# Where a 6 MB table of bucket lines is written to memory, in a two-block transformer kernel

## What is computed

```
for l in range(2):                              # first block
    h = rms_norm(x, pre_mix_norm[l]); proj = h @ w_in[l]
    mix = concat(neighbourhood(...), diff(...), gqa(...), mla(...)) @ w_o[l]
    x = x + rms_norm(mix, post_mix_norm[l])
    h = rms_norm(x, pre_ffn_norm[l])
    gate, up = split(h @ ffn_w_gate_up[l])
    x = x + rms_norm((silu(gate) * up) @ ffn_w_down[l], post_ffn_norm[l])
                                                # second block: attention with a bias by distance
bias = rel_table[rel_bucket(query - key)]       # 32 buckets, 16 heads
lg = q @ k.T * scale + bias                     # masked causally or to a band
```

## Time and profile before

| | us |
|---|---|
| median of 3 runs | 2453.93 (2448.55 to 2456.43) |
| profiled execution, device time | 2451.02 |
| its span | 2449.1 |
| PE busy | 2374.7 (97%) |
| DVE, ACT, POOL busy | 482.9, 387.4, 110.5 |
| HBM written, of 565.87 MB moved | 9.18 MB |

### The profile page before, as it was taken

The page is one execution under the profiler, slowest core; times in us unless marked ns, Lnnn a source line. Parts: engine busy times, 40 slices in busy tenths (PEclk is TensorE's granted clock), DMA queues, the critical chain, the costliest instruction groups (busy, mean ns, idle before and its releaser), DMA issues.

```text
span 2449.1 us, 34374 instructions
## 1 busy us (share of the span) xinstructions
PE 2374.7 (97%) x15191; PEld 1363.2 (56%) x15191; DVE 482.9 (20%) x1206; ACT 387.4 (16%) x951; POOL 110.5 (5%) x190
## 2 busy tenths in 40 slices
PE   7999999999999999999999988999999999999997
PEld 4777775778675767877676663333333333333332
DVE  3340002341001532200114431011101010111012
ACT  1420000241000252100015221111111111111110
POOL 3210100010000020100001000000000000000000
PEclk9999999999999999999999999999999999999999
DMA  9567633624425254342444346999999999999993
GB/s 296 206 65 193 230 120 116 244 67 146 166 102 184 83 215 155 134 172 103 135 144 148 112 146 237 382 389 337 369 393 378 347 367 391 374 353 369 391 371 150
DMA packets 245575, 568.15 MB, mean 232 GB/s; under 512 B 10336, under 2 KB 22816, under 8 KB 245424
## 3 DMA queue, kind: packets, MB, share of 16 engines
q1 hardware_dynamic: 233392, 532.24, 59.4%
q0 software_dynamic: 12032, 33.67, 6.0%
HBM read 556.69 MB, written 9.18 MB: 231 GB/s over the span
## 4 chain that ended last, share of the span: by engine, by line
PE 94%; DVE 2%; ACT 2%; issue 1%; DMA 1%; DVEq 0%; POOL 0%; SPq 0%; ACTq 0%
PE ps_d L1374 16%; PE ps_x L1401 8%; PE ps_s L1374 8%; PE ps_a L1163 8%; PE ps_d L1163 8%; PE ps_a L969 6%; PE ps_a L944 6%; PE ps_x L1180 5%; PE ps_s L1180 5%; PE ps_x L1407 4%; PE ps_s L1012 3%; PE ps_x L1012 3%; PE ps_x L1079 3%; PE ps_a L1147 2%; PE ps_d L1147 2%; PE ps_a L1061 1%
## 5 line engine op out<-in xcount | busy, mean ns | idle before, releaser
L1401 PE MATMUL ps_x<-slots,PT 128*32 128x512 f32 x1792 | 212.9, 593 | 0.8 <-ACT PT L1795 0.8
L1163 PE MATMUL ps_a<-hT,slots 128*128 128x256 f32 x864 | 192.7, 382 | 3.9 <-issue 3.9
L1374 PE MATMUL ps_d<-slots,hT 128*32 128x512 f32 x1792 | 195.8, 593 | 0.6 <-ACT hT L1745 0.6
L1374 PE MATMUL ps_d<-slots,N 128*32 128x512 f32 x1792 | 196.0, 593 | 0.0
L1163 PE MATMUL ps_d<-hT,slots 128*128 128x256 f32 x864 | 190.9, 379 | 0.0
L1163 PEld LDWEIGHTS ps_a<-hT,slots 128*128 128x128 f32 x864 | 165.4, 192 | 31.6 <-issue 9.9
L1163 PEld LDWEIGHTS ps_d<-hT,slots 128*128 128x128 f32 x864 | 164.5, 190 | 22.0
L969 PE MATMUL ps_a<-hT,slots 128*128 128x256 f32 (+1 forms) x768 | 143.4, 348 | 1.9 <-ACT hT L1617 1.5
L2503 DVE TENSOR_TENSOR proj<-proj,ps_d 128x512 f32<-128x512 f32 x33 | 22.7, 687 | 596.4 <-PE ps_d L1163 525.1
L969 PEld LDWEIGHTS ps_a<-hT,slots 128*128 128x128 f32 x768 | 126.9, 192 | 18.7 <-issue 5.6
L1401 PEld LDWEIGHTS ps_x<-slots,PT 128*32 128x32 f32 x1792 | 58.3, 110 | 132.8 <-issue 132.8
(11 more groups left out here) (371 smaller groups left out, 2374.5 us busy)
## 6 DMA issues: line engine op xcount, KB each, us to landing
slots<-in_moe_w_gate SPq DMA_DIRECT2D x56, 2048.0 KB, 9.6
slots<-in_moe_w_up SPq DMA_DIRECT2D x56, 2048.0 KB, 10.9
slots<-in_moe_w_down SPq DMA_DIRECT2D x56, 2048.0 KB, 11.2
slots<-in_ffn_w_gate_up SPq DMA_DIRECT2D x20, 2048.0 KB, 11.2
slots<-in_ffn_w_down SPq DMA_DIRECT2D x10, 2048.0 KB, 9.0
slots<-in_w_in SPq DMA_DIRECT2D x8, 2048.0 KB, 9.2
slots<-in_ff_w_gate SPq DMA_DIRECT2D x5, 2048.0 KB, 9.0
slots<-in_ff_w_up SPq DMA_DIRECT2D x5, 2048.0 KB, 8.5
```

The lines of the kernel that those rows point to most:

```text
L1163: last = pe.matmul(b[:, f * S:(f + 1) * S], v[:, k, (f0 + f) * P:(f0 + f + 1) * P], hT[:, k, :], start=(k == 0), stop=(k == KD - 1))
L1374: last = pe.matmul(b[TILE * j:TILE * j + TILE, :], x_of[i][:, k, TILE * c:TILE * c + TILE], views[w][:, k, :], start=(k == 0), stop=(k == ...
L1401: last = pe.matmul(b0[TILE * j:TILE * j + TILE, :], mine(f + o, c), v[:, f + o, 512 * half:512 * half + 512], start=(first and o == 0), st ...
```

## The change

The entry `lines` of Pool's list is no longer made at the first feed-forward. It is made at the stage whose `diff` is the last layer, that is, the second layer's attention, behind that stage's biases. The two transfers, their sources, their targets and their semaphore stay as they are.

```
-                first_ffn = [kind for kind, _ in stages].index("ffn") if any(k == "ffn" for k, _ in stages) else -1
                 for n, (kind, s) in enumerate(stages):
-                    if n == first_ffn:
-                        todo.append(("lines", n, None))
                     if kind == "small":
                         todo.append(("small", n, s["l"]))
...
                     for b in sorted({j["bias"] for u in s.get("units", []) for j in u["jobs"] if j["bias"] is not None}):
                         todo.append(("bias", n, b))
+                    if s.get("diff") == DEPTH - 1:
+                        todo.append(("lines", n, None))
```

## The result

The changed kernel takes 2478.48 us (median of 4 runs, 2475.8 to 2483.13), the kernel before 2453.48 beside it. The ratio is 1.0099, with a 95% interval from 1.0081 to 1.0118: some 25 us slower; 2477 was forecast. The profiled execution went from a span of 2449.1 to 2474.0, +24.9.

What follows compares the result with a forecast made beforehand. TensorE (PE), 94% of the chain, was taken to bound the kernel. 28.6 + 1.9 - 5.8 = +24.7 us gave 2475.7 on the profiled execution, 2478.6 by the median; forecast 2477, range 2463 to 2494.

Steps and rivals of the forecast that it cites:

- Place and order: Pool issues the write about 486.5 us, after the second layer's last distance bias; vectors and `mem` queue behind and land late.
- the sum: Whole kernel: 28.6 us PE delay, plus 1.9 slow clock, minus 5.8 saved in the first feed-forward, +24.7 us.
- First feed-forward, -5.8: First layer's feed-forward: PE's 3.89 us wait at 242.44 and 1.92 us of slow matmuls after it both go.
- Stall, +28.6: Second layer's feed-forward starts at 586.9 instead of 558.27, since PE waits for the late `mem` and vector: +28.6 us.
- My list of what the changed profile would show: Expected signs: write issued about 486.5, vector near 88 us to landing, PE idle 554.7 to about 583, no wait at 242.
- Clock behind the wait, +1.9: After PE's wait before the second layer's feed-forward, a lower clock costs 1.9 us, as after the earlier short wait.
- No vector passed the write: Rival: vectors and `mem` behind the write land before 543, so no stall; 2445 or 2448 us; chance 0.06.
- The second transfer does not get faster in an empty place: Rival claimed the opposite: it spreads over all engines without weights, write ends at 549; 2449 to 2452 us; chance 0.05.
- My reading that it is slow because it runs on half of the engines: The write's second transfer, 8 lines, runs on 8 of 16 engines at half the rate, taking another 41 us.
- The larger stall: Rival: weights and write disturb each other more, `mem` lands after 600, PE waits 45 us or more; 2495 and above; 0.06.
- my upper bound: Largest PE delay, +42 us: 28.6, plus 5 for weights beside the write, plus 8 for SP's loads ahead of `mem`.

Runs made afterwards that it cites:

- the vector alone: Changed kernel with both gain vectors still behind the write on Pool's queue, but `mem` loaded by SP on its own queue: 2476.38 us, ratio 1.01.
- `mem` alone: Changed kernel with the write issued behind the second layer's two gain vectors and ahead of `mem`: 2475.47 us, ratio 1.0089.
- nothing urgent behind the write: Changed kernel with the two gain vectors issued ahead of the write and `mem` loaded by SP on its own queue: 2465.79 us, ratio 1.0052.

## Why the prediction was right

**Place and order: right.** The write at 481 (486.5 less what the first feed-forward gives back), the vector 86.2 us to landing, `mem` behind it, PE idle in front of the turn of `mem`. The two conditions that the sum named (the vector and `mem`, both late) were tested each by itself. Each nearly carries the loss: the feed-forward starts 3.3 us earlier with the vector alone, and PE waits 2.7 us less with `mem` alone. For the vector the reason is partly another than I gave: ScalarE's order holds up the turn of `mem` too.

**First feed-forward, -5.8: measured -5.8** there (no wait, and 1.92 us less for the 32 matmuls). The changed kernel's execution had come to it 0.8 us later than that of the kernel before, and its last distance bias is issued 5.6 us earlier (485.12 to 479.52). That the wait was the write's is confirmed twice: it goes when the write is made fast in its old place, and comes back one layer later with the write behind `mem`. In the time of whole runs the gain is not seen.

**Stall, +28.6.** PE's wait measured 22.4 us, and yet the feed-forward began where the sum puts it. The sum lets everything come 5.8 us earlier: `mem` lands at 583.2 - 5.8 = 577.4, and it landed at 577.2. The end of the output projection should have come 5.8 us earlier too, at 548.8. It came at 554.9, since PE lost 5.2 us in the attention beside the write: the gap of 2.29 us, one of 0.84, and slow clock behind them. The sum has nothing for that; this term is wrong. It changes the place where the time is lost and not the end, because PE starts again when `mem` has landed, whatever it lost before. Where the wait is short, as with nothing urgent behind the write, most of it shows in the time. My list of what the changed profile would show has the write at 486.5 and `mem` at 583, without the 5.8 us, so there the times are 6 us too late.

That `mem`'s landing comes out within 0.2 us is in part luck. The second transfer landed 84.4 us after its issue and not 87.2, and the vector and `mem` landed 2.9 and 10.8 us behind it, where I had 1.9 and 8.4.

**Clock behind the wait, +1.9: measured +1.7** (577.28 to 582.69 for what took 554.57 to 558.27). From Pool's last distance bias on, the measured terms are -5.6, then +5.8 to the end of the output projection, +22.4 and +1.7, together 24.3; the feed-forward begins 24.4 us later, and the span is 24.9 longer.

**The rivals.** No vector passed the write. The second transfer does not get faster in an empty place. My reading that it is slow because it runs on half of the engines was half wrong: it does run so, but on all of them it is no faster. The source's partitions set the rate, for both transfers; of the source as the limit the prediction had said that it was my reading, and the source on 128 partitions shows it. The larger stall did not come: `mem` landed 10.8 us behind the write, so the competing loads of SP cost at most 2.4 us beyond my sum, where my upper bound had 8.

**Not forecast:** the gaps in the attention. They sit at the same matmuls of L1048 in all five kernels that reach them at normal clock with the slow write beside (2.2 to 2.8 us), and in none of the seven without the slow write there; in the run with only the first transfer, where PE came to this point some 12 us late and at the lower clock, there is none. In all five, a packet of an instruction queue is carried within a microsecond of the gap's start (at 501.5 us in the changed kernel), and PE goes on some 2 us later. The kernel before carries such a packet beside the same matmuls, at 507 us, and PE does not stop. The packet itself takes no longer beside the write (0.9 us, 1.3 before). That the write delays the arrival of PE's instructions is a possible cause; it was argued from this, not tried, and what would be held up is not shown.

## What to carry to other kernels

Before a transfer is moved to a quiet place, list what is issued behind it on the same queue, up to the first thing that a busy engine waits for, and take the landing times of loads that already stand behind such a transfer in the trace. Look at the rate and not only at the engines' busy share: 102 GB/s at a share of 0.96 says that the source or the target is narrow, and a source spread over all partitions made the write 3.5 times faster, after which none of three places tried cost anything measurable. A gain of 5 us in 2450 is not to be trusted from one profile when the clock can take 10 in a stretch that nothing changed; look at the mean granted clock of every run.

## What the runs showed of the hardware that was not expected

- A write of 6.29 MB from 16 partitions (the last third from 8) takes 84 to 90 us in every place tried; from 128 partitions (the last third from 64) 23 to 26 us.
- Beside it a load on another queue is slow as well: 1 MB in 25.7 us (5.3 on Pool's queue without the write), 2 MB in 49.6 us; and SP's issuing instruction itself is held for up to 34.9 us (0.37 at that place without the write).
- Matmuls pause for 2.2 to 2.8 us in the middle of a series beside such a write, with nothing to wait for in the profile.
- The granted clock fell to the 1.2 GHz level for 14 to 24 us in a stretch in which PE was busy, in 4 of 13 profiled executions: in three in the second layer's attention, in one in the first layer's, behind an idle time of PE of 0.7 us.
